# A norm's scale applied after the product: the first tile behind four RMS norms is summed from the un-normed input

## The reference, cut to what matters

```python
def rmsnorm(x, gain):
    y = x * lax.rsqrt(jnp.mean(x * x, axis=-1, keepdims=True) + EPS)
    return y * gain

h = h + mixer(rmsnorm(h, ...))            # mixer ends in mix_out
h = h + swiglu(rmsnorm(h, norm_ffn))      # norm 1, product ffn_in
# second network, depth 2, each norm with a scale and a shift (per feature) that come from c
h = h + g * attention(rmsnorm(h) * (1 + s) + t)   # norm 2, products gq_k, gq_v, gq_q
h = h + g * conv_ffn(rmsnorm(h) * (1 + s) + t)    # norm 3, product fc_in[0]
h = h + g * hyena(rmsnorm(h) * (1 + s) + t)       # norm 4, product hy_in
h = h + g * conv_ffn(rmsnorm(h) * (1 + s) + t)    # norm 5, product fc_in[1]
out = rmsnorm(h, final)                           # norm 6
```

## Time and profile before

| | before |
|---|---|
| median of 3 runs | 3013.83 us |
| the profiled execution, its own time | 3012.66 us |
| its span, first to last instruction | 3010.9 us |
| mean granted TensorE clock | 0.968 of 2.4 GHz |
| TensorE busy | 2840.6 us (94%) |
| VectorE, ScalarE, GpSimd busy | 1338.5, 702.6, 1609.8 us |

### The profile page before, as it was taken

One profiled execution on the slowest core, in us unless ns is written; L12 is line 12 of the kernel. 1 busy time (PEld: TensorE's weight loads), 2 busy tenths in 40 slices (PEclk: granted clock), 3 DMA queues, 4 the chain that ended last, 5 costly groups with the idle time before them and its releaser, 6 DMA issues.

```text
span 3010.9 us, 40043 instructions
## 1 busy us (share of the span) xinstructions
PE 2840.6 (94%) x15635; PEld 2286.4 (76%) x15635; DVE 1338.5 (44%) x1957; ACT 702.6 (23%) x1076; POOL 1609.8 (53%) x1569
## 2 busy tenths in 40 slices
PE   7998998999989999999989999999999898999998
PEld 6897887789768877888865567888777465788886
DVE  5576653311450275343345634331086577433312
ACT  2275223532330002111015632110011222211100
POOL 5652114655146665666652236676586433677663
PEclk9998999999999999999999999999999999999999
DMA  3221000222002456655631013333233000233321
GB/s 111 84 69 36 2 2 29 84 71 70 29 29 84 154 175 189 190 180 180 206 118 43 29 42 84 98 98 99 84 102 99 21 18 14 84 84 98 104 96 66
DMA packets 291862, 260.17 MB, mean 86 GB/s; under 512 B 6537, under 2 KB 264182, under 8 KB 291436
## 3 DMA queue, kind: packets, MB, share of 16 engines
q1 hardware_dynamic: 287840, 248.53, 26.6%
q0 software_dynamic: 2416, 6.34, 0.7%
q10 hardware_dynamic: 1436, 2.96, 0.3%
HBM read 255.72 MB, written 2.10 MB: 86 GB/s over the span
## 4 chain that ended last, share of the span: by engine, by line
PE 81%; DVE 8%; issue 5%; DVEq 2%; ACT 2%; POOL 2%; DMA 1%; POOLq 0%; ACTq 0%; SPq 0%
PE ps L511 22%; PE ps L513 21%; PE ps L512 21%; DVE cv L2150 2%; PE ps L1607 1%; PE ps L1627 1%; PE ps L1536 1%; PE ps L1471 1%; PE ps L1461 1%; PE ps L1220 1%; PE ps L1451 1%; PE ps L1206 1%; PE ps L856 1%; PE ps L1227 1%; PE ps L1271 0%
## 5 line engine op out<-in xcount | busy, mean ns | idle before, releaser
L744 POOL CAST spl<-raw 128x512 fp32r<-128x512 f32 (+1 forms) x352 | 248.1, 705 | 691.1 <-PE ps L513 543.7
L511 PE MATMUL ps<-HSH,spl 128*128 128x512 f32 x1344 | 537.8, 400 | 31.0 <-DVE HSL L669 15.8
L746 POOL TENSOR_TENSOR spl<-raw,spl 128x512 fp32r<-128x512 f32 (+1 forms) x352 | 501.3, 1424 | 60.3 <-issue 10.5
L512 PE MATMUL ps<-HSL,spl 128*128 128x512 f32 x1344 | 529.3, 394 | 0.0
L513 PE MATMUL ps<-HSH,spl 128*128 128x512 f32 x1344 | 529.3, 394 | 0.0
L750 POOL TENSOR_TENSOR spl<-raw,spl 128x512 fp32r<-128x512 f32 (+1 forms) x352 | 479.8, 1363 | 51.9 <-issue 1.8
L511 PE MATMUL ps<-HNH,spl 128*128 128x264 f32 (+1 forms) x1152 | 369.4, 321 | 29.5 <-issue 5.7
L512 PE MATMUL ps<-HNL,spl 128*128 128x264 f32 (+1 forms) x1152 | 360.5, 313 | 0.0
L513 PE MATMUL ps<-HNH,spl 128*128 128x264 f32 (+1 forms) x1152 | 359.0, 312 | 0.0
L748 POOL CAST spl<-raw 128x512 fp32r<-128x512 f32 (+1 forms) x352 | 231.0, 656 | 215.3 <-PE ps L513 213.3
L511 PEld LDWEIGHTS ps<-HSH,spl 128*128 128x128 f32 x1344 | 255.8, 190 | 106.0 <-issue 38.6
(11 more groups left out here) (442 smaller groups left out, 4474.2 us busy)
## 6 DMA issues: line engine op xcount, KB each, us to landing
adw<-in_ada_w SPq DMA_DIRECT2D x96, 512.0 KB, 5.5
raw<-in_w_in SPq DMA_DIRECT2D x44, 1024.0 KB, 5.2
raw<-in_ffn_w_up SPq DMA_DIRECT2D x88, 512.0 KB, 5.0
raw<-in_w_ffn_in SPq DMA_DIRECT2D x44, 512.0 KB, 5.0
raw<-in_ffn_w_down SPq DMA_DIRECT2D x16, 1408.0 KB, 6.2
raw<-in_hy_w_in SPq DMA_DIRECT2D x12, 1024.0 KB, 5.1
raw<-in_w_ffn_out SPq DMA_DIRECT2D x8, 1408.0 KB, 6.9
raw<-in_w_branch_dn SPq DMA_DIRECT2D x8, 1024.0 KB, 5.1
```

The costliest lines, as they stand in the source:

```text
L511: pe.matmul(dst, w[0], x[0], start=first, stop=False)
L512: pe.matmul(dst, w[0], x[1], start=False, stop=False)
L744: pool.tensor_copy(hi[:, first, :], w[:, first, :])
L746: pool.tensor_tensor(lo[:, first, :], w[:, first, :], hi[:, first, :], ALU.subtract).then_inc(split_first, 1)
```

## The change

For norms 1, 3, 4 and 5 (`EARLY`) the first tile of the next product is summed on its own, from gain * H without 1/rms, in PSUM bank 1.
- ScalarE makes the high half of gain * H(k) behind each square (8 copies a norm), VectorE the low half behind the residual additions (`early_lo`, 8 a norm).
- TensorE (`pe_tile_early`) waits for all six sums of squares, makes blocks 0 and 1, then the norm's sum over partitions (`norm_pe`), then blocks 2 to 7. Where there is a shift (norms 3, 4 and 5) each block has two more matmuls of two columns, which sum W't in bank 3.
- VectorE's norm then runs as before for the other tiles, but y0 waits for the early tile's middle and y4 for its end (they overwrite what it reads). Behind low2 VectorE waits for the early tile and multiplies it by 1/rms (`early_scale`, with a reduction of the two columns where there is a shift). For norms 3 and 5 ScalarE adds the shift's product in place, ahead of its high half 4; for norm 4 it does so in the copy that it makes anyway.
- The pair is now tiles 1 and 2, on banks 2 and 0.
- The filter's small matmul in front of hy_in moves behind tile 2.
- Behind norm 2 VectorE splits the shift columns (four copies and four subtractions of 128x8).

POOL's and SP's programs are not changed.

```diff
+        def pe_tile_early(pe, gm, u, x):
+            pe.wait_ge(split_first, gm.u0 + 1)
+            pe.wait_ge(n_add, (KD - 2) * u)
+            for k in range(gm.kt):
+                if k == gm.mid:
+                    pe.wait_ge(split_ready, gm.u0 + 1)
+                if k == 2:
+                    norm_pe(pe, u)
+                pe.wait_ge(n_out, out_base(u) + k + 1)
+                mm = products(pe, ps[:, EARLY_BANK, :], halves_of(gm, 0, k), x(k), k == 0, k == gm.kt - 1)
+                if EARLY[u]:
+                    l, n = {3: (0, 1), 4: (1, 0), 5: (1, 1)}[u]
+                    for part in range(2):
+                        mm = pe.matmul(ps[:, BIAS_BANK, 0:2], halves_of(gm, 0, k)[part], shift_col[:, l, n, k, :],
+                                       start=k + part == 0, stop=k == gm.kt - 1 and part == 1)
+                if k == gm.mid - 1:
+                    mm.then_inc(acc_half, 1)
+            mm.then_inc(acc_ready, 1)
...
-                for t, k in ((0, step), (1, step - LAG)):
+                for t, k in ((at, step), (at + 1, step - LAG)):
...
-                        pe.wait_ge(acc_free[b], gm.free(t))
+                        pe.wait_ge(acc_free[b], gm.free(0 if t == 2 else t))
...
+        EARLY = {1: False, 3: True, 4: True, 5: True}
+        BIAS_IN_PLACE = (3, 5)
+        EARLY_BANK, BIAS_BANK, SCALED_BEHIND, BIASED_BEHIND = 1, 3, 3, 4
...
                     act.activation(dst, x(k), ACT.Square).then_inc(n_sq, 1)
+                    if u in EARLY:
+                        act.activation(HSH[:, k, :], x(k), ACT.Copy, scale=norm_gain(u, k)).then_inc(n_hi, 1)
...
+                if u in BIAS_IN_PLACE and k == BIASED_BEHIND:
+                    act.wait_ge(n_out, scaled(u))
+                    tile_0 = ps[:, EARLY_BANK, :]
+                    act.activation(tile_0, tile_0, ACT.Identity, bias=early_bias[:, :], scale=1.0).then_inc(n_hi, 1)
...
+        def early_lo(dve, u, k):
+            dve.wait_ge(n_hi, hi_base(u) + k + 1)
+            dve.scalar_tensor_tensor(HSL[:, k, :], H[:, k, META:T], norm_gain(u, k), HSH[:, k, :], ALU.mult, ALU.subtract)\
+                .then_inc(n_out, 1)
+
+        def early_scale(dve, u, gm):
+            dve.wait_ge(acc_ready, gm.ready(0))
+            if EARLY[u]:
+                dve.tensor_reduce(early_bias[:, :], ps[:, BIAS_BANK, 0:2], AX.X, ALU.add)
+            tile_0 = ps[:, EARLY_BANK, :]
+            dve.tensor_tensor(tile_0, tile_0, NRS[:, 0:SEQ], ALU.mult).then_inc(n_out, 1)
...
                 ins.then_inc(n_out, 1)
+                if u in EARLY and k == SCALED_BEHIND - 1:
+                    early_scale(dve, u, gm)
             dve.wait_ge(n_rs, u + 1)
             for k in range(KD):
+                if u in EARLY and k == 0:
+                    dve.wait_ge(acc_half, gm.u0 + 1)
+                if u in EARLY and k == gm.mid:
+                    dve.wait_ge(acc_ready, gm.ready(0))
...
-                    if ready and i + r == 0:
-                        pe_tile_pair(pe, gm, x, ready, second=second)
+                        if early and n < 2:
+                            if n == 0:
+                                pe_tile_early(pe, gm, early, x)
+                            else:
+                                pe_tile_pair(pe, gm, x, ready, at=1)
...
-            norm_pe(pe, 4)
-
-            pe.wait_ge(y_in, 64)
-            pe.matmul(ps[0:FW, 7, :], W1[:, :], POS[:, :], start=True, stop=True).then_inc(y_mlp, 1)
...
                         if n == 0:
-                            pe_tile_pair(pe, hy_in, x_hn, lambda k: (n_out, 4 * KD + k + 1))
-                        elif n > 1:
+                            pe_tile_early(pe, hy_in, 4, x_hn)
+                        elif n == 1:
+                            pe_tile_pair(pe, hy_in, x_hn, n_ready(4), at=1)
+                        elif n > 2:
                             pe_tile(pe, hy_in, i, r, m, x_hn)
+                        if n == 2:
+                            pe.wait_ge(y_in, 64)
+                            pe.matmul(ps[0:FW, 7, :], W1[:, :], POS[:, :], start=True, stop=True).then_inc(y_mlp, 1)
...
+                    if u in EARLY and 1 <= t < KD - 1:
+                        early_lo(dve, u, t - 1)
+                if u in EARLY:
+                    early_lo(dve, u, KD - 1)
...
             shift_dve(dve, 2, 0, 0)
+            for l in range(2):
+                for n in range(2):
+                    x = mod[:, l, n * 3 * KD:n * 3 * KD + KD]
+                    dve.tensor_copy(shift_col[:, l, n, :, 0], x)
+                    dve.drain()
+                    dve.tensor_tensor(shift_col[:, l, n, :, 1], x, shift_col[:, l, n, :, 0], ALU.subtract)
```

More of the change, by code:

```diff
@@ L164, in build @@
         pcol = fresh("pcol", PT, P)
+        shift_col = at("shift_col", [2, 2, KD, 2], here[0] + P, dtype=F32R)
+        early_bias = at("early_bias", [1], here[0] + P + 4 * KD * 2)
         square = fresh("square", 8 * P + META)
@@ L611, in build, with out_base, hi_base, out_at @@
         LN_EXP, SILU = "natural_log_exp_and_others", "silu_and_others"
+        EARLY = {1: False, 3: True, 4: True, 5: True}
+        BIAS_IN_PLACE = (3, 5)
+        EARLY_BANK, BIAS_BANK, SCALED_BEHIND, BIASED_BEHIND = 1, 3, 3, 4
+        def out_base(u):
+            return sum(2 * KD + 1 if v in EARLY else KD for v in range(u))
+        def hi_base(u):
+            return sum((2 * KD if v in EARLY else KD) + (v in BIAS_IN_PLACE) for v in range(u))
+        def out_at(u, k):
+            return out_base(u) + k + 1 + (KD + (k >= SCALED_BEHIND) if u in EARLY else 0)
+        def hi_at(u, k):
+            return hi_base(u) + k + 1 + (KD if u in EARLY else 0) + (u in BIAS_IN_PLACE and k >= BIASED_BEHIND)
+        def scaled(u):
+            return out_base(u) + KD + SCALED_BEHIND + 1
+        def biased(u):
+            return hi_base(u) + KD + BIASED_BEHIND + 1
+        def norm_gain(u, k):
+            if u == 1:
+                return col("norm_ffn", k)
+            l, n = {2: (0, 0), 3: (0, 1), 4: (1, 0), 5: (1, 1)}[u]
+            return gsc[:, l, n, k:k + 1]
         def norm_act(act, u, x, n, shift=None, hi=True, tile=None):
@@ L693, in head_pe, with pe_gemm @@
             mm.then_inc(h_sum, 1)
-        def pe_gemm(pe, gm, x, ready=None, after=None, second=None):
+        def pe_gemm(pe, gm, x, ready=None, after=None, second=None, early=None, after_slab=None):
             for i, slabs in (turns_of(gm) if ready else groups(pe, gm)):
                 for r in slabs:
-                    if ready and i + r == 0:
-                        pe_tile_pair(pe, gm, x, ready, second=second)
-                    else:
-                        for m in range(2):
+                    for m in range(2):
+                        n = i * (2 * R) + 2 * r + m if ready else R
+                        if early and n < 2:
[3 more added lines that the diff above has]
+                                pe_tile_pair(pe, gm, x, ready, at=1)
+                        elif ready and not early and n == 0:
+                            pe_tile_pair(pe, gm, x, ready, second=second)
+                        elif n > 2 or n == 2 and not early:
                             pe_tile(pe, gm, i, r, m, x)
@@ L1378, in _, with ffn_ada @@
             pe_gemm(pe, mix_out, lambda k: (MGH[:, k, :], MGL[:, k, :]), lambda k: (merged, k + 1), ada_after(mix_out))
[L1380 to L1389, removed]
+            def ffn_ada(n):
+                for c in ada_units(ffn_in, n % R):
+                    ada_pe(pe, n // R, c)
+            pe_gemm(pe, ffn_in, x_hn, n_ready(1), early=1, after_slab=ffn_ada)
             x_act = lambda k: (AFH[:, k, :], AFL[:, k, :])
@@ L1517, in pe_conv_ffn @@
             def pe_conv_ffn(l, u):
-                norm_pe(pe, u)
-                pe_gemm(pe, fc_in[l], x_hn, lambda k: (n_out, u * KD + k + 1))
+                pe_gemm(pe, fc_in[l], x_hn, n_ready(u), early=u)
                 pe_gemm_pair(pe, fc_out[l], x_act, lambda q: (f_split, (l + 1) * KF + KF // (2 - q)))
             pe_conv_ffn(0, 3)
-            norm_pe(pe, 4)
-            pe.wait_ge(y_in, 64)
-            pe.matmul(ps[0:FW, 7, :], W1[:, :], POS[:, :], start=True, stop=True).then_inc(y_mlp, 1)
             even_odd = lambda x, n: x.rearrange("p (h i e) -> p e h i", e=2, h=2)[:, n // 2, n % 2, :]
@@ L2039, in _ @@
                     b = acc_in(act, hy_in, i, t)
-                    act.activation(UP[:, t % 2, 1:SEQ + 1], ps[:, 2 * b, :], ACT.Copy).then_inc(acc_free[b], 1)
+                    if n == 0:
+                        act.activation(UP[:, 0, 1:SEQ + 1], ps[:, EARLY_BANK, :], ACT.Identity, bias=early_bias[:, :], scale=1.0)\
+                            .then_inc(acc_free[b], 1)
+                    else:
+                        act.activation(UP[:, t % 2, 1:SEQ + 1], ps[:, 2 * b, :], ACT.Copy).then_inc(acc_free[b], 1)
                     if n == 2:
@@ L2576, in dve_conv_ffn @@
             def dve_conv_ffn(l, u):
-                shift_dve(dve, u, l, 1)
```

(3 more changed lines are left out.)

45 lines of the change are left out of this document (29 added, 16 removed).

## The result

| | before | after |
|---|---|---|
| median (runs on the same chip) | 3015.56 us (7) | 3025.44 us (7) |
| lowest to highest | 3013.30 to 3018.58 | 3018.97 to 3033.27 |
| the profiled execution, its span | 3012.66, 3010.9 | 3018.97, 3017.1 |
| last product before the norm to tile 3 of the next: norm 1 | 26.00 | 26.38 |
| norm 3 | 26.37 | 26.83 |

The ratio is 1.0036, 95% interval 1.0026 to 1.0046: the change makes the kernel slower by 8 to 14 us. None of the four norms gains; they lose 0.38 + 0.46 + 11.27 + 0.57 = 12.7 us. (Norm 1 is counted from the eight one-column matmuls, the first of which starts 0.23 us behind the last product.) (The profiled execution after is the fastest of the seven; why it is only 6 us over the one before is told behind experiment 12.)

A forecast was written before the change was run, and what follows sets the result against it. TensorE, busy 94%, was taken as the bound, with its gaps around the norms deciding. Norms 1, 3, 5 and 4 summed as -2.7 - 1.0 - 1.0 + 7.4 = +2.7 on 3013.83, giving 3016.5 us; range 3006 to 3025.

The forecast's parts named there:

- Rival B: All four norms: VectorE and POOL take turns wholly, 1.4 us per half split, perhaps clock loss; 3022 to 3026, chance 0.18.
- Norm 4, the queue moved past: Ahead of hy_in: the norm's sum now waits behind blocks 0 and 1 and POOL's split; +7.4 us (+6.4 to +8.4).
- rival C: Norm 4: POOL's wait before its subtraction comes from VectorE, now idle, so +3.3 instead of +7.4; 3006.8 to 3012.4, chance 0.17.
- plus 9.0 for 13 groups: Norm 4: from low3 at 2207.2, TensorE's remaining 13 groups take 9.0 us, to 2216.2.
- As the rows lie on both ends I take the middle: All four norms: a half split costs VectorE 0.85 us, between 0.34 and 1.4; three inside a norm, 2.5 us.
- Norms 3 and 5, the start and the chain: VectorE's norm starts 1.3 us late, its chain frees bank 2 at 1830.9, 1833.4 with POOL; -1.0 us each.
- 13 groups remain, 8.9: Norm 3: after low3 at 1822.6 TensorE needs 8.9 us for 13 groups, to 1831.7, ahead of VectorE's chain.
- Norm 1: Last addition up to 1.4 us late, 1/rms 1.3 late, VectorE's chain ends at 1182.8; tile 3 moves -2.7 us.
- At nothing: The shift columns behind norm 2, under 8.14 us of idle, and ScalarE's copies cost no time.
- Rival D: The early tile gains nothing at norms 1, 3 and 5, leaving only +7.4 us; 3021.2, chance 0.10.

The follow-up runs named there:

- experiment 12: The kernel before with only the filter's small matmul moved behind tile 2 of hy_in, no early tile: 3013.78 us, ratio 0.9996.
- experiment 6: The kernel after with the weights of tiles 2 and 3 behind the norms split on one column of 128 only: 3011.24 us, ratio 0.9981.
- experiment 5: The kernel after with POOL's split of tile 2 also held until VectorE's low 2: 3028.46 us, ratio 1.0041.
- experiment 7: The kernel after without early tiles, the seven filter transfers issued on ScalarE's queue behind norm 4: 3001.50 us, ratio 0.9954.

## Why the prediction was wrong

It forecast 3016.5, a difference of 2.7 us and "same"; the medians differ by 9.9, and 3025.44 lies above its range of 3006 to 3025. (The miss of the range is narrow: the median before was 3013.83 in three runs and is 3015.56 in seven, and taken as a difference the range ended at +11.2, with 9.9 inside it. The steps below failed all the same.) Rival B happened, with both its parts: a half split costs VectorE 1.33 us where B put 1.4, and the clock comes down behind the norms. Its price for the four norms was +12.1, measured +12.7; that these are so near is in part luck, as norm 1 was put at -1.3 in it and came at +0.4, and the clock behind norm 4 at 3.6 and came at 2.3.

- **Norm 4, the queue moved past: right, its size too small.** Forecast +7.4, measured +11.3. y0 was forecast at 2198.5 and came at 2198.91; POOL's subtraction at 2188.79 and came at 2188.89, with VectorE idle, so rival C is false. What was missing lies behind y0: 22.1 us to tile 3 where 18.6 were forecast. Two half splits cost 1.33 and not 0.85 each (1.0). And "plus 9.0 for 13 groups", a step that failed too, was at full clock, while the clock was 0.50 from 2208.5 to 2213: 4.5 us at half speed do 2.25 us of work, so 2.3 more. Together 3.3 of the 3.5.
- **"As the rows lie on both ends I take the middle": the step that failed at the other three.** It put a half split at 0.85 us; it costs 1.33 (experiment 6), near the upper end. The row that gave 0.34 was misread. VectorE's last two low halves there end at 1823.87, 0.40 us into POOL's subtraction, whose row before is this:

```profile
1823.47 1.55 POOL L746 TENSOR_TENSOR spl<-raw,spl 128x512 fp32r<-128x512 f32 x1
```

Until then POOL's cast had been the one to wait (2.61). So most of the half split had nothing of VectorE's left to slow, and the row says nothing of the price of a whole one. Nor is 1.42 the time without POOL: that is two y, while the last two low halves take 1.62 with POOL idle (1827.47 after). Three half splits are 4.0 us a norm and not 2.5.
- **Norms 3 and 5, the start and the chain: right.** y0 was forecast 5.87 us behind the last product and came at 5.78 and 5.77. The chain without contention was to free the bank at 1830.9, 22.9 behind the last product; experiment 6, nearly without contention, frees it at 22.7 and has tile 3 at 22.82. With 4.0 of contention that is 26.9, measured 26.83. So +0.5 each for -1.0. That tile 3 would wait for VectorE is in norm 5's row and in experiment 5's.
- **"13 groups remain, 8.9": wrong.** They took 11.4 (1822.92 to 1834.34), four of them at half clock. At norm 3 this costs nothing, as VectorE's chain ends within 0.1 us of them.
- **Norm 1: two terms too small, and TensorE last by a little.** Forecast -2.7, measured +0.4. y0 is 2.5 us later behind the last product (6.81 against 4.32) for 1.3 forecast, since the last addition is 2.5 late behind it and not up to 1.4; three half splits at 1.33 give 1.5 more, and the last 0.4 is TensorE's, which ends behind VectorE here. Experiment 6 shows 21.54 nearly without POOL's work.
- **At nothing:** right as far as the runs show. The two-column matmuls lengthen a group from 0.69 to 0.92, 0.23 for the 0.27 taken. The small matmul's move is 0.9, as forecast (experiment 12).
- **Rival D** (no gain at norms 1, 3, 5) names what was measured there, 0.4 to 0.6, by another cause: the start is late by 1.2 at norms 3 and 5, as forecast, but it's the half splits that take the gain.
- The Trainium skill, "SBUF — State Buffer", section "Who interferes with whom", says that a VectorE instruction with two SBUF inputs and a GpSimd one that reads SBUF shut each other out. The rows agree with that side: y is 1.76 where it is 0.74, POOL's subtraction 1.54 where it is 1.28. Its strict reading, 1.9 us per half split, was too high: 1.33 measured, so 0.6 us of POOL's cast and subtraction cost VectorE nothing; which part of them isn't shown.

## What to carry to other kernels

An instruction moved to the front of a queue brings its waits with it: ask of each what it waits for, and what behind it used to run in that wait. When two engines slow each other, price the overlap by a row in which both work from start to end, and not by one where either stops. And before an idle stretch is filled with new work, look whether what causes it can be moved: here seven transfers on another queue made the norm 4.5 us shorter (and the median 13.7, the rest by a stage whose two lengths aren't explained), and with the early tiles on top of that all four norms were longer again.

## What the runs showed of the hardware that was not expected

- POOL idles 2.85 to 6.63 us between a cast and the subtraction behind it, where transfers were issued on it just before, with VectorE idle too (4.69 after), and not at all without them (experiment 7). Why isn't shown. The same seven transfers take ScalarE's queue 3.9 us to issue in experiment 7.
- TensorE came down to half clock behind norm 3 though it never sat idle there for over 1.4 us: from 1816 to 1824 it was busy 5.3 us, its matmuls take 0.63 from 1821.33 on, and they still do so until 1828.1, though it had all its work from 1822.92; the windows of norm 3 after show it (0.65, 0.50, then 1.00).
- The hyena stage has two lengths, 404.1 and 411.6 us in the mean, in kernels that differ ahead of it. They go with whether VectorE's and POOL's streams meet; that this causes them isn't shown. The 7.5 us between them is more than the 6 us that were taken as what a measurement can tell. One profiled execution can't show a change of that size; the lengths of the touched stretches can, though one of them too moved by 0.8 in an untouched norm (experiment 12).
